# Attention scores from rounded parts: three one-pass products in place of one fp32 product, in a two-block transformer kernel on one Trainium2 core

## The chip, the core and the metric

The kernel runs on one core of one Trainium2 chip. The metric is the device time of one execution in microseconds (us), lower is better. Engines are called as in the profile: PE is the matrix engine (TensorE), PEld its weight loads, DVE the vector engine, ACT the scalar engine, POOL the GpSimd engine, SP the engine whose queue issues most of the DMAs.

## What is computed

The reference is a chain of two transformer blocks on a sequence of 512 tokens with 1024 channels, all in fp32: an attention layer with forget gates and 16 heads of 64 (the "first attention"), an attention layer with a sliding window, then a second block with three mixers and an MLP. The change touches one product of the first attention, the logits:

```python
u = rmsnorm(h, norm_a_g[i])
proj = u @ w_in_a[i]
q, k, v, f_logit, gate = jnp.split(proj, ...)
q = rmsnorm(q.reshape(b, s, N_HEADS_A, HEAD_DIM), qnorm_a_g[i])
k = rmsnorm(k.reshape(b, s, N_HEADS_A, HEAD_DIM), knorm_a_g[i])
...
logits = jnp.einsum('bqhd,bkhd->bhqk', qi, k) * scale
logits = logits + ci[..., :, None] - c_k[..., None, :]
logits = jnp.where(causal, logits, -jnp.inf)
p = jax.nn.softmax(logits, axis=-1)
return jnp.einsum('bhqk,bkhd->bqhd', p.astype(v.dtype), v)
```

## The kernel before

Everything is kept transposed in SBUF: channels on the 128 partitions, the 512 tokens along the free dimension. The kernel is written by hand, one instruction stream for each engine, with semaphores between them; so the order of the work on an engine is the order in which its function calls the helpers.

A projection is done in units. A unit is 128 output channels: 8 contraction tiles of 128, and for each three products, because both operands are split into a rounded part (type fp32r, which PE multiplies in one pass) and a rest (the value less its rounded part, also fp32r): high by high, high by low, low by high (`gemm`, L868 to L870). The weights of a unit are loaded by SP, rounded by ACT (`split_hi`, L1953) and their rest is formed by DVE (`split_lo`, L2456) or POOL (L498).

The first attention works on pairs of heads, n = 0 to 7; head 0 of a pair lies on partitions 0 to 63, head 1 on 64 to 127. For each pair m four units are projected: queries, keys, values, gate. DVE scales them out of PSUM (`scale_a`, L1203); ACT squares the queries and keys (L1993), PE sums the squares within a head, ACT and DVE form the inverse root (`root_scalar`, L576 to L579; `rsqrt_vector`, L584 and L586), and DVE multiplies by it (`normed_a`, L926), into `qn` and `kn`, the two halves of tile `qkv`. The semaphore `a_qk` counts these. Then come the scores, in three rounds (`scores_a`, L995 and L998): round 0 is query block 3 against 512 keys, round 1 query block 2 against 384 keys, round 2 query block 1 against 256 keys and query block 0 against 128. Each round writes one PSUM bank for each head, `S[0]` and `S[1]`:

```python
A_ROUND = [[(3, 0, 4 * P)], [(2, 0, 3 * P)], [(1, 0, 2 * P), (0, 2 * P, P)]]
mm(S[h][:, at:at + w], qn[lo:hi, q * P:(q + 1) * P], kn[lo:hi, 0:w], start=(i == 0), stop=False)
```

The operands of this product are fp32 with 64 contraction rows. A bf16 product adds the causal mask (L998). DVE adds the forget gate's terms and takes the lowest value of each row (`logits_a`, L1010), ACT takes the exponentials (`exps_a`, L1023), PE transposes them (`turn_a`, L1035), ACT copies the transposes out of PSUM (`take_turned_a`, L1046), and PE multiplies them by the values (`mix_a`, L1056).

While PE works on the scores of pair n it also projects pair n + 1: between two steps of the attention always stands half a unit (4 contraction tiles, 12 products) or two halves. The order on PE for a pair is: half a unit; scores round 0; two halves; scores round 1; transposes of round 0; half a unit; mixing of round 0; half a unit; scores round 2; transposes of round 1; half a unit; mixing; half a unit; transposes of round 2; half a unit; mixing; spreading of the softmax's sums (`spread_a`, L1078); transposing the values (`turn_v`, L1436). In the last pair, n = 7, there is no next pair to project; only the gate's unit and the first units of the output projection (`output_a`) stand between the steps.

On ACT the end of a pair is: `root_scalar` for the keys of pair n + 1, `take_turned_a(n, 2)`, `split_hi` of a unit, and the DMA of the forget gate's terms for a later pair (`load_c`). On DVE it is: `normed_a` for the queries of pair n + 1 behind `logits_a(n, 2)`, `scale_a` for the values, a `split_lo`, `normed_a` for the keys, another `split_lo`, and a piece of other work: in pairs 0 to 3 a part of the rotary angles, in pairs 4 to 7 a block of the second block's modulation (`ada_block`, L985). The next pair on DVE begins with `scale_a` of the gate's unit, the copy of the transposed values (L2535), a `split_lo`, and `logits_a` of round 0. Pair 0 has a preamble of its own, in which the same steps stand without a previous pair.

`normed_a` writes `qn` and `kn` in place, one buffer each. So it waits until the scores of the previous pair are done (`a_scores` at 6 m).

## Time and profile before

| | |
|---|---|
| runs | 1260.44 us median of 3 (1259.88 to 1260.48) |
| profiled execution | span 1259.4 us; 1.0 us below the median of the runs, which also holds what lies around the span |
| PE | busy 1244.9 us, 99% of the span |
| DVE, ACT, POOL | busy 56%, 53%, 29% |
| first attention's pairs | scores of pair 0 begin at 39.3 us, those of pair 7 at 269.1 us; 33.2 us for a pair |

How to read it: PE is called busy from the first to the last of its matmuls' records, and a matmul's record is longer than its share of the engine, since matmuls are pipelined. So the time that a matmul costs is read from the distance between the starts of two that follow each other, not from its duration. DVE and ACT records also overlap a little with the next one. Every time below is counted from the span's start.

### The profile page before, as it was taken

To read this page: it belongs to the slowest core of one execution; us is meant where nothing else is said; L and a number is where in the kernel's file an instruction comes from. 1 tells how busy PE (TensorE), PEld (TensorE's weight loads), DVE (VectorE), ACT (ScalarE), POOL (GpSimd) and SP (SyncE) were. 2 spreads that over 40 slices of the span, in tenths; PEclk is the share of its full clock that TensorE was granted. 3 is DMA by queue.
4 is the path that set the end of the run, shared out by engine and by line. 5 is a ranking of instruction groups with operands and counts; after the bars stand their busy time and mean duration, and the time that the engine had idled before them with its cause. 6 is when DMAs were issued, how large, how long until landed. Compare 5 with 4: busy or idle time off the path is not lost.

```text
span 1259.4 us, 19239 instructions
## 1 busy us (share of the span) xinstructions
PE 1244.9 (99%) x7192; PEld 1003.7 (80%) x7192; DVE 702.1 (56%) x1486; ACT 672.4 (53%) x1278; POOL 370.2 (29%) x191
## 2 busy tenths in 40 slices
PE   9999999999999999999999999999999999999998
PEld 8777777778877777689676888888988888888887
DVE  6766667775575766565798546684662121221223
ACT  6766666675437676635567886753542242331331
POOL 0000000004310000054487774123255344353450
PEclk9999999999999999999999999999999999999999
DMA  5322243343332322253222022331363233232232
GB/s 204 107 67 85 84 158 126 119 134 117 100 90 97 101 84 85 83 184 92 68 84 84 18 68 69 117 135 50 102 217 116 71 115 101 84 109 92 84 100 68
DMA packets 38411, 128.11 MB, mean 102 GB/s; under 512 B 4640, under 2 KB 7584, under 8 KB 38320
## 3 DMA queue, kind: packets, MB, share of 16 engines
q1 hardware_dynamic: 35792, 121.91, 30.3%
q10 hardware_dynamic: 2528, 4.98, 1.1%
q8 instruction: 58, 0.95, 0.3%
q14 instruction: 33, 0.27, 0.1%
HBM read 123.43 MB, written 2.13 MB: 100 GB/s over the span
## 4 chain that ended last, share of the span: by engine, by line
PE 80%; ACT 6%; issue 6%; DVE 5%; DMA 1%; POOL 1%; ACTq 0%; DVEq 0%; SPq 0%; POOLq 0%
PE G L868 19%; PE G L870 19%; PE G L869 19%; ACT scr L1249 2%; PE S L1708 2%; PE S L995 2%; PE O L1056 2%; DVE wL L2456 1%; PE T L1035 1%; ACT wH L1953 1%; DMA w<-weights_dram 1%; PE S L1726 1%; PE N L1078 1%; PE G L840 1%; PE G L841 1%
## 5 line engine op out<-in xcount | busy, mean ns | idle before, releaser
L498 POOL TENSOR_TENSOR wL<-w,wH 128x1024 fp32r<-128x1024 f32 x119 | 290.2, 2443 | 831.1 <-ACT wH L1953 831.0
L868 PE MATMUL G<-hi,wH 128*128 128x512 f32 x1208 | 487.1, 403 | 0.5 <-DVE xT L963 0.4
L870 PE MATMUL G<-hi,wL 128*128 128x512 f32 x1208 | 472.5, 391 | 0.0
L869 PE MATMUL G<-lo,wH 128*128 128x512 f32 x1208 | 472.1, 391 | 0.0
L868 PEld LDWEIGHTS G<-hi,wH 128*128 128x128 f32 x1208 | 227.6, 188 | 56.6 <-issue 9.7
L1953 ACT ACTIVATE wH<-w 128x1024 fp32r<-128x1024 f32 x170 | 179.2, 1055 | 170.6 <-PE G L870 111.3
L870 PEld LDWEIGHTS G<-hi,wL 128*128 128x128 f32 x1208 | 227.3, 188 | 49.9
L869 PEld LDWEIGHTS G<-lo,wH 128*128 128x128 f32 x1208 | 228.0, 189 | 44.8 <-issue 1.2
L965 DVE SCALAR_TENSOR_TENSOR xT<-G,modT,xT 128x512 f32<-128x512 f32 x34 | 25.5, 751 | 124.9 <-PE G L870 124.9
L2456 DVE TENSOR_TENSOR wL<-w,wH 128x1024 fp32r<-128x1024 f32 x51 | 62.3, 1222 | 42.3 <-ACT wH L1953 41.5
L2428 ACT ACTIVATE tmp<-G 128x512 f32<-128x512 f32 x31 | 18.6, 600 | 119.7 <-PE G L870 116.1
L2981 DVE TENSOR_TENSOR T<-tmp,G 128x512 f32<-128x512 f32 x31 | 21.6, 696 | 94.5 <-ACT tmp L2428 94.5
L985 DVE CUSTOM_DVE_ANT_0 adaw<-adaw,scr 128x1024 f32<-128x1024 f32 x31 | 51.1, 1649 | 1.9 <-issue 1.7
L1023 ACT ACTIVATE scr<-scr,sa 128x256 f32<-128x256 f32 (+2 forms) x64 | 35.2, 558 | 26.9 <-DVE sa L1010 26.9
L1249 ACT ACTIVATE scr<-S,bs,bq 128x128 f32<-128x128 f32 (+1 forms) x64 | 33.6, 534 | 21.5 <-DVE bs L1239 21.5
L2985 DVE TENSOR_TENSOR lo<-T,hi 128x512 fp32r<-128x512 f32 x32 | 22.1, 692 | 26.5 <-ACT hi L2435 26.5
L2809 DVE TENSOR_TENSOR kd<-S,qkv 128x512 f32<-128x512 f32 x24 | 16.5, 689 | 31.1 <-ACT S L2256 27.1
L1010 DVE CUSTOM_DVE_ANT_0 scr<-S,kd 128x256 f32<-128x256 f32 (+2 forms) x64 | 28.6, 487 | 0.0
L1046 ACT ACTIVATE scr<-T 128x384 f32<-128x384 f32 (+1 forms) x48 | 22.7, 526 | 10.4 <-PE T L1035 9.9
L533 POOL TENSOR_TENSOR tmp<-tmp,rms 128x482 f32<-128x482 f32 (+19 forms) x20 | 24.4, 1222 | 11.2 <-ACT rms L2173 11.2
L2774 DVE MAX8 best<-adaw 128x8 f32<-128x256 f32 (+2 forms) x48 | 26.7, 557 | 0.8
L533 POOL TENSOR_TENSOR tmp<-tmp,rinv 128x482 f32<-128x482 f32 (+19 forms) x20 | 23.8, 1190 | 7.8 <-ACT rinv L2173 7.8
(461 smaller groups left out, 1923.9 us busy)
## 6 DMA issues: line engine op xcount, KB each, us to landing
w<-weights_dram SPq DMA_DIRECT2D x170, 512.0 KB, 3.6
adaw<-ada_dram SPq DMA_DIRECT2D x43, 512.0 KB, 4.3
kd<-c_dram ACTq DMA_DIRECT2D x8, 512.0 KB, 3.7
cbias<-ada_dram SPq DMA_DIRECT2D x5, 512.0 KB, 4.3
xT<-x_dram SPq DMA_DIRECT2D x4, 512.0 KB, 8.0
out_dram<-xT SPq DMA_DIRECT2D x8, 256.0 KB, 2.6
scr<-ca_dram SPq DMA_DIRECT2D x2, 512.0 KB, 4.9
kd<-cbias SPq DMA_DIRECT2D x8, 128.0 KB, 3.2
```

The source lines that it names most:

```text
L498: g.tensor_tensor(wL[:, u.slot], w32[:, u.slot % 2], wH[:, u.slot].bitcast(f32), ALU.subtract).then_inc(w_lo, 1)
L533: g.tensor_tensor(cacc[:, n % 2, back:SEQ], cacc[:, n % 2, back:SEQ], term[n % 3][:, 0:SEQ - back], ALU.add).then_inc(sem("conv_added"), 1)
L868: mm(home[:, :], whi, H[:, k, :], start=(k == first), stop=False)
L869: mm(home[:, :], whi, L[:, k, :], start=False, stop=False)
L870: last = mm(home[:, :], wlo, H[:, k, :], start=False, stop=(k == final))
L985: v.tensor_tensor_reduce(out=home, in0=home, in1=copy, scale=1.0, scalar=0.0, op0=ALU.mult, op1=ALU.add, accum_out=modsum[:, b.n:b.n + 1]) ...
L1010: v.tensor_tensor_reduce(out=slot[:, h * 512 + at:h * 512 + at + w], in0=S[h][:, at:at + w], in1=kd[:, n % 2 * 2 + h, 0:w], scale=-1.0, sc ...
L1023: s.activation(part, part, ACT.Exp, bias=sa[:, n % 2, LOW, h, q:q + 1], scale=-1.0, accum_out=sa[:, n % 2, ASUM, h, q:q + 1]).then_inc(sem ...
L1249: s.activation(pb[:, h * 512 + at:h * 512 + at + w], S[h][:, at:at + w], ACT.Exp, bias=st[:, NEGM, h, q:q + 1], scale=bq[:, n % 2, ROOT, h ...
L1953: s.activation(wH[:, u.slot], w32[:, u.slot % 2], ACT.Copy).then_inc(w_hi, 1)
L2456: v.tensor_tensor(wL[:, u.slot], w32[:, u.slot % 2], wH[:, u.slot].bitcast(f32), ALU.subtract).then_inc(w_lo, 1)
L2774: link(v.max(best[:, n % 2, :], part))
```

## The change

Each fp32 product of the scores becomes three products of fp32r operands, added up in the same PSUM bank: rounded queries by rounded keys, rests of the queries by rounded keys, rounded queries by rests of the keys. The product of the two rests is left out.

The rounded parts and the rests are made in two new tiles, `qk_hi` and `qk_lo` (128 x 2 x 512 each; index 0 the queries, 1 the keys). ACT rounds (`qk_high`), DVE subtracts (`qk_low`). `normed_a` no longer waits for the scores of the previous pair but for the rounding of it (`a_qk_hi`); the rounding waits for the scores (`a_scores`). PE waits for the last rest (`a_qk_lo`) in place of `a_qk`. The room for the two tiles comes from the area that is reserved for the descriptors of software-made DMAs, which is set to 1024.

```diff
+        qk_hi, qk_lo = sb("qk_hi", [P, 2, SEQ], f32r), sb("qk_lo", [P, 2, SEQ], f32r)
...
         def scores_a(pe, n, r):
-            pe.wait_ge(sem("a_qk"), 2 * n + 2)
+            pe.wait_ge(sem("a_qk_lo"), 2 * n + 2)
             wait(pe, sem("a_logits"), 8 * n + 2 * r)
             for i, (q, at, w) in enumerate(A_ROUND[r]):
-                for h in range(2):
-                    lo, hi = h * DH, (h + 1) * DH
-                    mm(S[h][:, at:at + w], qn[lo:hi, q * P:(q + 1) * P], kn[lo:hi, 0:w], start=(i == 0), stop=False)
+                for part, (a_q, a_k) in enumerate(((qk_hi, qk_hi), (qk_lo, qk_hi), (qk_hi, qk_lo))):
+                    for h in range(2):
+                        lo, hi = h * DH, (h + 1) * DH
+                        mm(S[h][:, at:at + w], a_q[lo:hi, 0, q * P:(q + 1) * P], a_k[lo:hi, 1, 0:w], start=(i == 0 and part == 0),
+                           stop=False)
...
+        def qk_high(act, m, which):
+            act.wait_ge(sem("a_qk"), 2 * m + which + 1)
+            wait(act, sem("a_scores"), 6 * m)
+            s.activation(qk_hi[:, which, :], [qn, kn][which], ACT.Copy).then_inc(sem("a_qk_hi"), 1)
+
+        def qk_low(dve, m, which):
+            dve.wait_ge(sem("a_qk_hi"), 2 * m + which + 1)
+            v.tensor_tensor(qk_lo[:, which, :], [qn, kn][which], qk_hi[:, which, :].bitcast(f32), ALU.subtract
+                            ).then_inc(sem("a_qk_lo"), 1)
...
             root_scalar(act, link, "a", 0, 1)
+            qk_high(act, 0, 0)
...
             load_c(0)
             split_a(2)
+            qk_high(act, 0, 1)
             load_c(1)
...
                     root_scalar(act, link, "a", n + 1, 1)
+                    qk_high(act, n + 1, 0)
                 take_turned_a(act, n, 2)
                 if more:
                     split_a(6 + 4 * n)
+                    qk_high(act, n + 1, 1)
...
             def normed_a(m, which, src, dst):
-                normed_vector(dve, link, "a", m, which, src, dst, which, mark("a_scores", 6 * m), sem("a_qk"))
+                normed_vector(dve, link, "a", m, which, src, dst, which, mark("a_qk_hi", 2 * m - 1 + which), sem("a_qk"))
...
             split_a(2)
+            qk_low(dve, 0, 0)
+            qk_low(dve, 0, 1)
...
                     normed_a(n + 1, 1, kraw, kn[:, :])
+                    qk_low(dve, n + 1, 0)
                     split_a(6 + 4 * n)
+                    qk_low(dve, n + 1, 1)
...
-    nc = bacc.Bacc("TRN2", target_bir_lowering=False, num_devices=1)
+    nc = bacc.Bacc("TRN2", target_bir_lowering=False, num_devices=1, dynamic_dma_scratch_size=1024)
```

The order on DVE ahead of the first scores, before (`normed_a` of the keys of pair 0 is the row with `kraw`; wL is the weights' rest, `cact` a small vector; line numbers of the profile):

```order
L926 SCALAR_TENSOR_TENSOR qkv<-kraw,vecT,rinv 128x512 [waits dve_link]
L2526 TENSOR_TENSOR cact<-vecT,cth 128x8 [waits c_sigmoid]
L2456 TENSOR_TENSOR wL<-w,wH 128x1024 [waits gemm_done,w_hi]
L2529 CAST pair_r<-pair 128x128 [waits const_here]
L2535 COPY qkv<-T 128x512 [waits a_vturn,dve_link]
```

And now:

```order
L927 SCALAR_TENSOR_TENSOR qkv<-kraw,vecT,rinv 128x512 [waits dve_link]
L2543 TENSOR_TENSOR cact<-vecT,cth 128x8 [waits c_sigmoid]
L2473 TENSOR_TENSOR wL<-w,wH 128x1024 [waits gemm_done,w_hi]
L1011 TENSOR_TENSOR qk_lo<-qkv,qk_hi 128x512 [waits a_qk_hi] x2
L2548 CAST pair_r<-pair 128x128 [waits const_here]
L2554 COPY qkv<-T 128x512 [waits a_vturn,dve_link]
```

The first scores used to be free once the first of these rows was done; now they are free behind both rests, which stand after a split of weights.

The order on DVE at the end of pair 6, from the keys of pair 7 on, before:

```order
L926 SCALAR_TENSOR_TENSOR qkv<-kraw,vecT,rinv 128x512 [waits a_scores,dve_link]
L2456 TENSOR_TENSOR wL<-w,wH 128x1024 [waits gemm_done,w_hi]
L984 MEMSET stat 128x1 [waits ada_here0,cactb_here]
L985 ISA adaw,modsum<-adaw,cbias 128x1024
L985 ISA modsum 128x1
L1203 TENSOR_TENSOR zraw<-G,tmp 128x512 [waits a_silu,gemm_done]
L2535 COPY qkv<-T 128x512 [waits a_vturn]
L2456 TENSOR_TENSOR wL<-w,wH 128x1024 [waits gemm_done,w_hi]
L882 SCALAR_TENSOR_TENSOR th<-zraw,th 128x512 [waits a_softplus]
```

And now (behind the last row `logits_a(7, 0)` follows in both):

```order
L927 SCALAR_TENSOR_TENSOR qkv<-kraw,vecT,rinv 128x512 [waits a_qk_hi,dve_link]
L1011 TENSOR_TENSOR qk_lo<-qkv,qk_hi 128x512 [waits a_qk_hi]
L2473 TENSOR_TENSOR wL<-w,wH 128x1024 [waits gemm_done,w_hi]
L1011 TENSOR_TENSOR qk_lo<-qkv,qk_hi 128x512 [waits a_qk_hi]
L985 MEMSET stat 128x1 [waits ada_here0,cactb_here]
L986 ISA adaw,modsum<-adaw,cbias 128x1024
L986 ISA modsum 128x1
L1216 TENSOR_TENSOR zraw<-G,tmp 128x512 [waits a_silu,gemm_done]
L2554 COPY qkv<-T 128x512 [waits a_vturn]
L2473 TENSOR_TENSOR wL<-w,wH 128x1024 [waits gemm_done,w_hi]
L883 SCALAR_TENSOR_TENSOR th<-zraw,th 128x512 [waits a_softplus]
```

Two instructions of 512 columns have come in ahead of everything that DVE does for pair 7, one of them behind a wait for ACT.

The first scores on PE, before:

```order
L995 MATMUL S<-qkv 128x512 [waits a_qk]
L995 MATMUL S<-qkv 128x512
L998 MATMUL S<-band,identb 128x128 x2
```

And now:

```order
L997 MATMUL S<-qk_hi 128x512 [waits a_qk_lo]
L997 MATMUL S<-qk_hi 128x512
L997 MATMUL S<-qk_hi,qk_lo 128x512 x2
L997 MATMUL S<-qk_lo,qk_hi 128x512 x2
L1001 MATMUL S<-band,identb 128x128 x2
```

One product of each head has become three, and the two heads alternate within each.

## Rows read from the trace of the kernel before

**Rows 1.** The page: busy time of the engines, and PE's granted clock in 40 slices.

```profile
PE 1244.9 (99%) x7192; PEld 1003.7 (80%) x7192; DVE 702.1 (56%) x1486; ACT 672.4 (53%) x1278; POOL 370.2 (29%) x191
PEclk9999999999999999999999999999999999999999
```

**Rows 2.** Busy time by stretch: us, PE, PEld, DVE, ACT, POOL, clock, DMA; one pair.

```profile
72.00:105.00 33.00, 33.00 (x197) 25.25 (x195) 22.26 (x52) 22.13 (x44) 0.00 (x0) 1.00 0.25 81
```

**Rows 3.** Timeline of PE in pair 1: start us, busy us, engine, line; three rounds of scores.

```profile
72.54 0.30 PEld L995 LDWEIGHTS S<-qkv 64*128 64x128 f32 x4 [0.35 <-issue]
72.54 1.13 PE L995 MATMUL S<-qkv 64*128 64x512 f32 x4
73.60 0.28 PE L998 MATMUL S<-band,identb 128*128 128x128 bf16 x2
...
74.02 0.39 PE L869 MATMUL G<-lo,wH 128*128 128x512 f32 x1
74.25 0.39 PE L870 MATMUL G<-hi,wL 128*128 128x512 f32 x1
...
79.35 0.92 PE L995 MATMUL S<-qkv 64*128 64x384 f32 x4
80.20 0.29 PE L998 MATMUL S<-band,identb 128*128 128x128 bf16 x2
...
88.47 0.92 PE L995 MATMUL S<-qkv 64*128 64x256 f32 x8
89.33 0.40 PE L998 MATMUL S<-band,identb 128*128 128x128 bf16 x4
```

**Rows 4.** Timeline of PE elsewhere: fp32r products of 256 columns, transposes of 128.

```profile
80.32 1.04 PE L1035 MATMUL T<-ident,scr 128*128 128x128 f32 x8
...
570.97 0.28 PE L840 MATMUL G<-hi,wH 128*128 128x256 f32 x1
571.09 0.28 PE L841 MATMUL G<-hi,wL 128*128 128x256 f32 x1
```

**Rows 5.** Timeline ahead of the first scores: ACT, DVE and PE.

```profile
36.50 1.06 ACT L1953 ACTIVATE wH<-w 128x1024 fp32r<-128x1024 f32 x1 [0.16 <-issue]
...
38.27 0.75 DVE L926 SCALAR_TENSOR_TENSOR qkv<-kraw,vecT,rinv 128x512 f32<-128x512 f32 x1
...
39.02 1.22 DVE L2456 TENSOR_TENSOR wL<-w,wH 128x1024 fp32r<-128x1024 f32 x1
...
39.30 1.13 PE L995 MATMUL S<-qkv 64*128 64x512 f32 x4
40.15 0.22 DVE L2529 CAST pair_r<-pair 128x128 fp32r<-128x128 f32 x1
```

**Rows 6.** Groups by line and shape: the same rounding and subtraction elsewhere; busy, mean ns.

```profile
L943 ACT ACTIVATE hi<-og 128x512 fp32r<-128x512 f32 x16 | 10.1, 633 | 22.8 <-DVE og L1401 20.0 <-DVE og L1087 2.8
L947 DVE TENSOR_TENSOR lo<-og,hi 128x512 fp32r<-128x512 f32 x16 | 11.0, 686 | 1.4 <-ACT hi L943 1.4
```

**Rows 7.** Timeline at the end of pair 2: keys of pair 3, and its scores.

```profile
98.72 0.75 DVE L926 SCALAR_TENSOR_TENSOR qkv<-kraw,vecT,rinv 128x512 f32<-128x512 f32 x1
...
105.77 1.13 PE L995 MATMUL S<-qkv 64*128 64x512 f32 x4
```

**Rows 8.** Timeline from the keys of pair 7 to its last scores: DVE, ACT, PE.

```profile
264.85 0.75 DVE L926 SCALAR_TENSOR_TENSOR qkv<-kraw,vecT,rinv 128x512 f32<-128x512 f32 x1
...
269.25 0.69 DVE L2535 COPY qkv<-T 128x512 f32<-128x512 f32 x1 [0.55 <-PE T L1436]
...
273.06 0.71 ACT L1023 ACTIVATE scr<-scr,sa 128x512 f32<-128x512 f32 x1
...
274.22 1.04 PE L1035 MATMUL T<-ident,scr 128*128 128x128 f32 x8
...
278.11 0.55 DVE L1010 CUSTOM_DVE_ANT_0 scr<-S,kd 128x384 f32<-128x384 f32 x1
...
278.98 0.92 PE L995 MATMUL S<-qkv 64*128 64x256 f32 x8
```

## The prediction

> **What bounds the kernel now.** I read the page first. PE is busy for 99% of the span and its granted clock is full, 2.4 GHz, in all 40 slices [rows 1]; no other engine passes 56%. Then the stretch of one pair of heads: PE is busy for all of its 33 us, DVE for 22.3, ACT for 22.1 [rows 2]. So in the first attention every us that PE's work loses is a us of the kernel, and every us that PE is made to wait is one too; work on DVE and ACT costs nothing as long as nobody on PE waits for it. The rest is therefore three questions: what the scores cost on PE, at which of the eight pairs PE would wait for the new steps, and what lies hidden.
>
> **The products on PE.** The two heads of a pair lie on different halves of the rows, and their products run side by side: four records, each longer than half a us, fit into 1.13 us [rows 3]. What counts is the distance from the first score to the mask's product behind it: 1.06 us in round 0 (73.60 less 72.54), 0.85 in round 1 (80.20 less 79.35), 0.86 in round 2 (89.33 less 88.47) [rows 3]. Rounds 0 and 1 differ by 128 columns and 0.21 us, 1.64 ns a column, which is four columns' time at 2.4 GHz (0.417 ns): an fp32 product streams its columns four times. What is left, 1.06 less 512 x 1.64 ns, is 0.2 us a round that doesn't depend on the columns: 0.1 ahead of it, 0.1 behind.
>
> The new product is three one-pass products. Their price is bounded from two sides. At best each costs one pass, 0.417 ns a column, so each round saves one pass of its columns: 0.21 us, 0.16 us, and in round 2 (384 columns) 0.16. At worst each costs what an fp32r product with all 128 rows costs now from start to start: 0.23 us for 512 columns [rows 3], 0.12 for 256 [rows 4], so about 0.175 for 384, and for 128 columns 0.11, the step of the transposes of 128 columns ((1.04 less 0.27, the length of one) / 7) [rows 4]. With 0.2 us around them that makes 0.89, 0.73 and 0.89 us: savings of 0.17, 0.12 and -0.03. So a pair saves between 0.26 and 0.53 us. I take 0.20, 0.15 and 0.02, **0.37 us a pair**: the small parts of round 2 are nearest to the rows with 0.12 and 0.11, the wide ones lie between, since the first gap and the last hold one pass each and not a whole step.
>
> The transposes' step shows that 128 columns cost 0.11 us, twice their columns' time. The Trainium skill has another number: on its page "TensorE: Matmul & The Clock Gate", section "Back-to-back issue gap", the gap of a single warm matmul is its columns at 2.4 GHz and 2.5 ns, which gives 56 ns at 128 columns. By that round 2 would save 0.16 us more a pair and the sum below would be lower by about 1.1 us; the rows decide here.
>
> **The new steps on ACT and DVE.** Sixteen roundings of 0.63 us on ACT and sixteen subtractions of 0.69 us on DVE [rows 6], 1.3 and 1.4 us for a pair of 33.2 in which each has some 11 us free [rows 2]. In the middle pairs they are hidden: the keys of pair 3 are ready at 99.47 and its scores begin at 105.77 [rows 7], 6.3 us later. Behind the keys now come a rest (0.7), a split of weights that already stood there (1.2) and a second rest (0.7), and ACT rounds the keys (0.6) while DVE splits; ready some 2.5 us after the keys, 3.8 us ahead of need. Pairs 1 to 6 cost PE nothing, I say. ACT's transposes' copy behind the rounding of the queries moves by 0.1 us at most, since ACT waited half a us for PE there.
>
> **Pair 0** has no such slack. The keys are ready at 39.02 and PE starts the scores at 39.30, as soon as its previous product lets it [rows 5]. Now DVE first splits weights from 39.02 on, as before; the instruction behind the split starts at 40.15 [rows 5], and that is now the first rest; the second follows after 0.61 to 0.69 us and takes 0.69. So the last rest is there at 41.45 to 41.55. ACT is no later: it splits at 36.5 for 1.06 us [rows 5], 0.6 later than that now, is free by 38.2, and rounds the keys from 39.06 to 39.7. PE starts at about 41.5 in place of 39.30: **2.2 us lost** (2.1 to 2.5), nothing is behind it that PE could take up meanwhile, because its stream is in order. DVE's copy of the values and ACT's later work are not late by that: they are ahead of a PE that is itself 2.2 us later.
>
> **Pair 7** is the other tight place, since PE has little to do between its steps. The two rests push DVE by 1.2 us from 265.6 on. DVE had some waits there, 0.55 us for PE's transposes [rows 8] among them, but the gate's chain over ACT (from `zraw`) runs beside that wait and isn't absorbed as far; I reckon that `logits_a(7, 0)` comes 0.8 us later. Before, the exponentials ended at 273.8 (with the read of their sum 273.9) and the transposes began at 274.22, right behind PE's own work [rows 8]: slack 0.35. PE now arrives 0.35 us sooner (its savings in rounds 0 and 1), so it waits 0.8 us: those savings are gone and 0.45 us more. Next, the logits of round 1 ended at 278.7 and the scores of round 2 began at 278.98 [rows 8]; DVE is 0.8 later and PE 0.45, another 0.1. Behind that DVE waits for PE again. **Pair 7 loses 0.5 us** against before (0.1 to 0.9), and gains only the 0.02 of round 2.
>
> **Edits at nothing.** The smaller area for DMA descriptors: POOL has no DMA of its own in this program, so no queue changes. The wait of `normed_a` for the roundings of the previous pair in place of its scores: both are over long before. SP's and POOL's streams are untouched; the DMAs that ACT issues (`load_c`) stand behind the rounding of the keys and move by about 1.5 us, with a whole pair in which to land. If the cover in pairs 1 to 6 were gone, each would cost what it is late by.
>
> **The sum.** Seven pairs save 0.37 us, 2.6 in all; pair 0 gives back 2.2, pair 7 0.5. Against the profiled execution: 1259.4 - 2.6 + 2.2 + 0.5 = 1259.5 us span, and the median of the runs lies 1.0 above the span: **1260.5 us, no change**. The bounds: 7 x 0.53 saved against 2.1 and 0.1 lost gives -1.5; 7 x 0.26 against 2.5 and 0.9 gives +1.6. So 1258.9 to 1262.1.
>
> **The rivals.**
>
> *The halves don't run side by side in this type.* No row has fp32r products with 64 rows. If the two heads' products came one after another, each round would hold six in place of three: 6 x 0.23 and 0.2 is 1.58 against 1.06, 6 x 0.175 and 0.2 is 1.25 against 0.85, 6 x 0.12 + 6 x 0.11 and 0.2 is 1.58 against 0.86: 1.64 us more a pair. Times eight, and 2.2 for pair 0 (pair 7's waits vanish in it): +15.3, **1275.7 us, slower**. It decides as soon as the two heads' starts lie a step apart. Against it speaks that fp32, and the same kernel's other products on part of the rows, do run side by side. Chance 0.08.
>
> *Weight loads that can't run ahead.* An fp32 product is two loads and two matmuls. All four loads of round 0 take 0.30 us in all, while its matmuls run for 1.06 [rows 3]: the second loads are done before the second matmuls start. If fp32r's loads had to wait for the matmul on the same rows, two loads in round 0, two in round 1 and five in round 2 would stand bare, at about 0.1 us each (half of the 0.2 us around a round): 0.9 us a pair, +7.2 on the sum less the 0.5 that pair 7 then hides: **1267.2 us, slower**. The Trainium skill has this rule, same page, section "The mechanism": weight loads overlap running matmuls only on other row groups. The trace of the fp32 scores disagrees with it, by the 0.30 us. Chance 0.07.
>
> *Narrow fp32r products cost more than one pass.* Nothing in the trace is fp32r and narrower than 256 columns. If the 128 columns of round 2 cost four passes each as fp32 does, 0.21 in place of 0.11, a pair costs 0.3 us more: +2.4, **1262.9 us**, on the border of slower. Chance 0.06.
>
> *The wait at pair 0 is shorter.* If ACT and DVE overlap better than the starts say, and every product costs one pass, the saving may come through: 8 x 0.53 less 1.5 is -2.7, **1257.7 us, faster**. The split at 39.02 would have to be quicker than in each of its other records. Chance 0.05.
>
> *The clock falls.* The granted clock is full throughout [rows 1], and PE never pauses for 2 us once it has begun; the pause at pair 0 is new. Products at 1.2 GHz take twice as long; a few us of them would cost 2 to 3 us: **1263 us**. Chance 0.04.
>
> **How the numbers follow.** The forecast has 0.70. A measurement of this kernel can tell about 0.2% from no change, 2.5 us, so 1257.9 to 1263.0 is "the same". Within it lie the forecast's bounds, and about half of the third and the last rival. Faster: 0.05 and a little for errors in my waits, 0.06. Slower: 0.08 + 0.07 + half of 0.10, and the same for errors, 0.21. Same: 0.73. The range takes in the forecast and its bounds, the narrow products and the clock: 1258.2 to 1263.4, some 0.8 of the chance; only the two large slower cases and the ends lie outside.
>
> **What would show it.** Right: the distance from the first score to the mask's product falls to about 0.86, 0.70 and 0.84 us, with six records side by side; a wait of about 2.2 us of PE for `qk_lo` ahead of the first scores and for no other pair; about 32.9 us for a pair; a wait of 0.8 us of PE for ACT at 7's first transposes. Wrong: a round 0 of more than 1.06 us; starts of the two heads more than 0.1 us apart; a PE wait for `qk_lo` in pairs 1 to 7; a clock slice below full.

## The result, and the profile after

The changed kernel takes 1263.32 us (median of 18 runs, 1259.52 to 1267.46); the kernel before took 1260.47 us beside it (18 runs, 1258.47 to 1262.62). The ratio is 1.0025, 95% interval 1.0015 to 1.0034: **slower by 0.25%**, 3.2 us. Three more measurements of the unedited change (below) gave 1.0007, 1.0010 and 1.0011, so its mean over four is 1.0013, 1.7 us; the first was the highest of them. The profiled execution has a span of 1262.0 us at a mean granted clock of 0.996. Two executions of later experiments fell into a slow state (1903 and 1544 us, at clocks of 0.60 and 0.75) and are in no ratio or mean below.

The page of the changed kernel, answering to [rows 1]:

```profile
PE 1243.2 (99%) x7256; PEld 1008.3 (80%) x7256; DVE 711.8 (56%) x1502; ACT 680.3 (54%) x1294; POOL 370.0 (29%) x191
PEclk9999999999999999999999999999999999999999
```

PE is busy 1.7 us less than before in a span that is 2.6 us longer. The products are cheaper, then, and PE stands idle more.

**The products.** Timeline of PE and PEld in the changed kernel, pair 1 (columns as in [rows 3]); L997 are the scores, L1001 the mask:

```profile
74.47 0.50 PE L997 MATMUL S<-qk_hi 64*128 64x512 f32 x2
74.57 0.19 PEld L997 LDWEIGHTS S<-qk_hi,qk_lo 64*128 64x128 f32 x2
74.80 0.39 PE L997 MATMUL S<-qk_hi,qk_lo 64*128 64x512 f32 x2
75.03 0.39 PE L997 MATMUL S<-qk_lo,qk_hi 64*128 64x512 f32 x2
75.36 0.29 PE L1001 MATMUL S<-band,identb 128*128 128x128 bf16 x2
...
81.08 0.45 PE L997 MATMUL S<-qk_hi 64*128 64x384 f32 x2
...
81.81 0.28 PE L1001 MATMUL S<-band,identb 128*128 128x128 bf16 x2
...
90.07 0.39 PE L997 MATMUL S<-qk_hi 64*128 64x256 f32 x2
90.30 0.28 PE L997 MATMUL S<-qk_hi,qk_lo 64*128 64x256 f32 x2
90.41 0.27 PE L997 MATMUL S<-qk_lo,qk_hi 64*128 64x256 f32 x2
90.53 0.22 PE L997 MATMUL S<-qk_hi 64*128 64x128 f32 x2
90.58 0.27 PE L997 MATMUL S<-qk_hi,qk_lo 64*128 64x128 f32 x2
90.69 0.28 PE L997 MATMUL S<-qk_lo,qk_hi 64*128 64x128 f32 x2
90.90 0.40 PE L1001 MATMUL S<-band,identb 128*128 128x128 bf16 x4
```

From the first score to the mask: 0.89 us in round 0, 0.73 in round 1, 0.83 in round 2, where [rows 3] had 1.06, 0.85 and 0.86. Each "x2" is the two heads in one row, side by side. The first scores of pairs 1, 2 and 6 start at 74.47, 107.34 and 238.87: a pair takes 32.88 us ((238.87 less 74.47) / 5), where it took 33.23 (105.77 less 72.54, [rows 3, 7]; 105.77 is where pair 2 begins, not pair 3). That is 0.35 us saved a pair.

**The waits.** The same kernel's waits of PE from the start to 290 us (total, times, longest), and the timeline around them:

```profile
PE S L997 <- DVE qk_lo L1011: 2.1, 1, 2.1
PE N L1421 <- DVE epsc L2477: 1.1, 1, 1.1
PE S L997 <- DVE sa L1023: 0.7, 1, 0.7
```

```profile
39.05 1.22 DVE L2473 TENSOR_TENSOR wL<-w,wH 128x1024 fp32r<-128x1024 f32 x1
39.09 0.63 ACT L1007 ACTIVATE qk_hi<-qkv 128x512 fp32r<-128x512 f32 x1 [1.26 <-DVE qkv L927]
...
40.19 1.29 DVE L1011 TENSOR_TENSOR qk_lo<-qkv,qk_hi 128x512 fp32r<-128x512 f32 x2
...
41.53 0.50 PE L997 MATMUL S<-qk_hi 64*128 64x512 f32 x2 [2.13 <-DVE qk_lo L1011]
...
273.42 0.08 DVE L1023 DVE_READ_ACCUMULATOR2_ANT sa<- 128x1 f32 x1
...
273.65 0.44 PE L997 MATMUL S<-qk_hi 64*128 64x384 f32 x2 [0.66 <-DVE sa L1023]
...
274.49 1.04 PE L1048 MATMUL T<-ident,scr 128*128 128x128 f32 x8
...
279.40 0.39 PE L997 MATMUL S<-qk_hi 64*128 64x256 f32 x2
```

Pair 0's scores begin at 41.53 in place of 39.30 [rows 5], 2.23 us late, and `qk_lo` is waited for once in the whole kernel. (The 1.1 us at L1421 is in the kernel before too, under L1408.) In pair 7 PE waits 0.66 us for the logits of round 0 ahead of the scores of round 1. The scores of pair 7's round 2, the last that the change touches, begin at 279.40, where they began at 278.98 [rows 8]: **0.4 us late. The rest of the 2.6 us in this trace arises behind the first attention**, in work that the change doesn't touch.

Most of it arises at PE's sums of squares behind the output of the second attention. The waits of PE between 560 and 570 us, of the kernel before and of the changed one:

```profile
PE N L680 <- DVE rms L663: 0.2, 1, 0.2
```

```profile
PE N L681 <- DVE rms L664: 1.7, 1, 1.7
```

And the timeline of POOL, DVE and ACT ahead of them, again before and then changed:

```profile
559.17 2.74 POOL L498 TENSOR_TENSOR wL<-w,wH 128x1024 fp32r<-128x1024 f32 x1 [1.26 <-ACT wH L1953]
...
560.35 2.65 DVE L985 CUSTOM_DVE_ANT_0 adaw<-adaw,scr 128x1024 f32<-128x1024 f32 x1 [0.69 <-issue]
```

```profile
558.78 1.22 DVE L986 CUSTOM_DVE_ANT_0 adaw<-adaw,scr 128x1024 f32<-128x1024 f32 x1
...
560.15 1.06 ACT L1966 ACTIVATE wH<-w 128x1024 fp32r<-128x1024 f32 x1 [4.09 <-DMA w<-weights_dram]
...
561.29 2.41 POOL L499 TENSOR_TENSOR wL<-w,wH 128x1024 fp32r<-128x1024 f32 x1 [3.24 <-ACT wH L1966]
561.42 3.36 DVE L986 CUSTOM_DVE_ANT_0 adaw<-adaw,scr 128x1024 f32<-128x1024 f32 x1 [1.41 <-issue]
```

ACT waits 4.09 us for weights there. DVE's sum over a block of the modulation vector begins 1.1 us later, and beside POOL's subtraction it takes 3.36 us; the same instruction took 1.22 at 558.78. PE waits 1.7 us for what stands behind it, 1.5 more than before. Three more traces of the change (experiments 2, 11 and 14) have 3.4 us for this sum as well. In the first two of them it begins at 559.88 and 560.11, and PE waits 0.5 us. What is special to the trace here is the late start, behind the weights that ACT waited for.

With 0.4 and 1.5 us, 0.7 of the 2.6 are left. By the starts of the same products, the changed kernel is 2.1 us late at 815 us and 2.9 at 868; between the two PE's clock fell to 1.2 GHz at 860 us here, and at 823 in the trace of before. The second trace of the kernel before (experiment 1) has its fall at 857 too: against the first it is 0.4 us early at 815 and 0.4 late at 868, the same 0.8. So these 0.8 us are the place of a fall, which moves without the change as well.

### The profile page after: what moved, and what is told of

The parts are those of the page before. It is cut to its first block, busy times and chain, and to the rows that moved or that the text cites. A ratio compares the mean times of both kernels' runs of the same rounds, so it can differ in the third digit from the quotient of the medians.

```text
span 1262.0 us, 19413 instructions
## 1 busy us (share of the span) xinstructions
PE 1243.2 (99%) x7256; PEld 1008.3 (80%) x7256; DVE 711.8 (56%) x1502; ACT 680.3 (54%) x1294; POOL 370.0 (29%) x191
## 4 chain that ended last, share of the span: by engine, by line
PE 79%; ACT 7%; DVE 7%; issue 5%; POOL 1%; DMA 1%; ACTq 0%; DVEq 0%; POOLq 0%
PE G L869 19%; PE G L871 18%; PE G L870 18%; ACT scr L1262 2%; PE O L1069 2%; PE S L997 1%; PE S L1721 1%; PE T L1048 1%; DVE wL L2473 1%; ACT wH L1966 1%; PE S L1739 1%; PE N L1421 1%; POOL tmp L534 1%; PE G L841 1%; PE G L842 1%
## 5 line engine op out<-in xcount | busy, mean ns | idle before, releaser
L2796 DVE MATCH_REPLACE8 adaw<-best,adaw 128x256 f32<-128x256 f32 (+2 forms) x48 | 26.0, 543 | 0.0
```

## The experiments

All ratios are to the kernel before on the same chip, with their 95% intervals; us are the ratio times 1260.5.

**1 and 2: both kernels again, unedited.**

> The kernel before, once more, to have the granted clock of each of its executions. In the two traces the first attention differs by only 0.4 us, yet the medians differ by 2.9, and the executions of the changed kernel have clocks from 0.998 down to 0.994, the lower the longer. Theory 1 (the pause): the wait of 2.2 us at pair 0 lets the clock fall in part of the executions; then the kernel before has no execution below about 0.996, and its times lie within 1258.5 to 1262.6. Theory 2 (chance elsewhere: the clock falls later, near 730 to 860 us, whatever the first attention does): the kernel before shows 0.994 as often as the changed one, in about a third of its executions.

> The changed kernel once more. Ratio 1.0025 +- 0.001, clocks again between 0.998 and 0.994, with about 2 us for each 0.002. Theory 1: an execution of 0.994 has a stretch at half clock within some 10 us of the pause at 39 to 41.5 us, beside two later ones. Theory 2: none there. The wait of 1.7 us for DVE at 564 us (rms, L664) that the profile of the changed kernel shows and that of the kernel before doesn't: if it comes from where a load happens to land, it is there in one of two executions of either kernel; if it comes from the change, it is there again.

The kernel before: 0.9998 (0.9989 to 1.0007). Theory 1 wanted no execution of it below a clock of about 0.996, theory 2 wanted a third of them there. Of these 11 two are, of all 124 executions of the kernel before beside the experiments 14, of the change's 53 also 14: neither theory holds as it was put. The change: 1.0007 (0.9996 to 1.0017), its trace again with 2.1 us for `qk_lo` and 0.7 for `sa`; the wait at 565 us was 0.5 us in it, not 1.7. So that wait differs between executions of one kernel.

**3: the pause alone.** Pair 0's roundings, rests and PE's wait for them, put into the kernel before; all products stay fp32.

```diff
+            if n == 0:
+                pe.wait_ge(sem("a_qk_lo"), 2)
...
+            qk_low(dve, 0, 0)
+            qk_low(dve, 0, 1)
```

> The kernel before with the two new tiles, the smaller descriptor area and, for pair 0 alone, the two roundings and the two rests; PE waits for the last rest ahead of pair 0's first scores. All products stay fp32. Theory 1: span + 2.2 us for the pause and clocks down to 0.994 as in the changed kernel, some 2 us more in the middle: ratio about 1.0035. Theory 2: + 2.2 us alone and clocks as before: 1.0018.

Ratio 1.0025 (1.0014 to 1.0035), 3.2 us for a wait of 2.2 us in the trace: one us more than the trace puts at the pause, and between the two forecasts.

**4: the pause filled with products that nobody reads.** 9 fp32 products of 128 columns ahead of pair 0's first scores.

```diff
+                if n == 0:
+                    for _ in range(9):
+                        mm(T[1][:, 0:P], ones[:, :], ones[:, :], start=True, stop=True)
                 scores_a(pe, n, 0)
```

> The changed kernel with nine more products of ones (128 columns, fp32, into a bank that nobody reads then) on PE ahead of pair 0's scores, about 2.0 us of work in the place of the pause; they add no result. Theory 1: the pause is gone for the clock though not for the time: the first attention costs the same, and the executions at 0.994 vanish: ratio about 1.0003. Theory 2: the same 1.0025 as the changed kernel.

Ratio 0.9997 (0.9988 to 1.0006), though the scores begin at 41.53 as in the change.

**5: the tiles alone**, with nothing written to them, and the smaller descriptor area, in the kernel before.

> The kernel before with nothing but the two new tiles (unused) and the smaller area for DMA descriptors: memory layout alone. So far, executions of equal granted clock are some 1.3 us longer in the changed kernel, of which the trace puts 0.4 us into the first attention; the rest could be the wait of PE at 564 us (0.7 to 2.0 us in four traces with the new layout, 0.44 in two without). Theory 1 (the layout makes loads land later or DVE and POOL slower at 540 to 564 us): ratio 1.0007, and that wait is above 0.6 us. Theory 2 (chance of when loads land): ratio 1.0000 within 0.0008, wait 0.44.

Ratio 0.9999 (0.9990 to 1.0009), wait at 565 us 0.2 us as before: the layout costs nothing.

**6: the pause filled with useful work.** The second half of pair 1's query unit is moved ahead of pair 0's first scores.

```diff
-                    gemm_a(n + 1, 0, FIRST if n else range(2, 4))
+                    gemm_a(n + 1, 0, FIRST if n else range(2, KT))
...
-                    gemm_a(n + 1, 0, SECOND)
+                    if n:
+                        gemm_a(n + 1, 0, SECOND)
                     gemm_a(n + 1, 1, FIRST)
```

> The changed kernel with the second half of the queries' unit of pair 1 moved on PE from behind to ahead of pair 0's first scores: 12 products of 0.23 us, 2.7 us of real work in the 2.2 us pause. If the sum of the terms is right, the pause is gone and with it 2.2 us: first attention 0.4 - 2.2 = 1.8 us shorter than before, ratio 0.9986. If the changed kernel's loss lies elsewhere, it keeps +0.9 and the ratio is 0.9993. If the pause only moves (the scores' consumers are late instead), PE waits ahead of round 1.

Ratio 1.0004 (0.9995 to 1.0012). The trace does what was expected: no wait of PE for `qk_lo`, and round 2 of pair 7 at 277.20, 1.8 us ahead of before. The times don't show it. In its trace 0.6 us go again between 565 and 596 us, and PE runs at 1.2 GHz for longer around 735 us (granted clock of 730 to 745 us: 0.77, before 0.89). Over its 12 executions the mean granted clock is 0.9958, where the kernel before beside it has 0.9971: an estimate from this, 0.0013 of 1259 us, is 1.6 us lost to more stretches at 1.2 GHz, out of the 2.3 us that are missing. Both forecasts of the time missed. Why the clock falls more often here, where PE has no pause ahead of the scores, is **not explained**.

**7: pair 0 stays fp32**, without its roundings and rests.

```diff
+            if n == 0:
+                pe.wait_ge(sem("a_qk"), 2)
+            else:
+                pe.wait_ge(sem("a_qk_lo"), 2 * n)
```

> The changed kernel with pair 0's scores as fp32 products again, without roundings and rests for pair 0. The pause of 2.2 us goes, pair 0's saving of 0.35 goes too: first attention 0.4 - 2.2 + 0.35 = 1.45 us shorter than before, ratio 0.9988 (0.9995 if something outside keeps 0.9).

Ratio 0.9987 (0.9978 to 0.9996), 1.6 us faster than before; round 2 of pair 7 begins at 277.46, 1.5 us ahead.

**8: work in the pause as in 6, and pair 7 in fp32**, without its roundings and rests.

> fill_gemm with pair 7's scores as fp32 products, and no roundings and rests for pair 7. Seven pairs save 0.35 us each and nothing is given back: 2.4 us shorter than before, ratio 0.9981. If pair 7's waits are not from the two rests on DVE, it is like fill_gemm less the saving: 0.9989.

Ratio 0.9988 (0.9980 to 0.9997). Its trace has no wait of PE for `sa`, and round 2 of pair 7 at 276.42, 2.6 us ahead of before: the wait in pair 7 comes from that pair's roundings and rests, and goes with them. The times again keep less, 1.5 us: they fit the forecast for the case that the wait has another cause (0.9989), and the trace speaks against that case. Here the mean clock, 0.9969 against 0.9971, doesn't explain the difference.

**9 and 10: the modulation blocks spread evenly**, in the change and in the kernel before.

```diff
-ADA_PER = {"b": (ADA_OB, (0, 1, 1, 1, 1, 2))}
+ADA_PER = {"b": (ADA_OB, (1, 1, 1, 1, 1, 1))}
```

> The change, with one edit far behind it: the six blocks of the modulation vector that VectorE sums beside the output of the second attention are spread evenly (one per output tile, where the last tile had two and the first none), so that at 558 to 565 us one block instead of two stands ahead of the add that TensorE's sums wait for. In the traces taken so far that wait is 0.2 us in kernels that save time ahead of it or change nothing, 1.7, 0.5, 1.2 and 0.4 us in those with the change's pause. Theory A (the rest of the loss lies in this wait, which the first attention's 0.4 us only sets off): the wait reads about 0.2 us, the ratio to the kernel before is 1.0003, and the trace is less than 1 us behind that of before at 600 us. Theory B (the loss has another home, stretches at 1.2 GHz that come more often): the wait is gone as well, but the ratio stays at 1.001 to 1.0025. Theory C (nothing systematic lies behind the first attention): ratio 1.0003 here and for the change run again.

> The kernel before with the same edit of the blocks alone. It has 0.2 us of that wait to lose, so all theories expect no difference that can be measured: ratio 0.9995 to 1.0003. A slower time would say that the even spread costs something of its own (a load of a block waited for, earlier in the output), which would then have to be taken off the result of the run above.

The change so edited: 1.0013 (1.0002 to 1.0024); the kernel before so edited: 1.0002 (0.9992 to 1.0011). The wait at the sums is gone in both, but an earlier block now holds up a sum that PE needs; the waits of PE between 530 and 570 us have this row in the changed kernel and its like in the other:

```profile
PE G L869 <- DVE xT L964: 1.3, 1, 1.3
```

So one wait took the place of another, and theory A, by which the rest of the loss is that wait at 565 us, isn't supported. It isn't refuted either, since a wait of the same size was left; in the kernel before, 1.3 us of it cost 0.3 us by the ratio, which is within the noise. What this trace shows beside it is new. Its timeline of PE has the first scores at 41.5 us as before, but these stretches (columns as in [rows 2], the clock third from the end):

```profile
40.00:42.00 2.00, 0.51 (x4) 0.46 (x6) 1.97 (x5) 0.94 (x1) 0.00 (x0) 1.00 0.91 276
42.00:43.00 1.00, 1.00 (x7) 0.37 (x6) 1.00 (x2) 0.12 (x1) 0.00 (x0) 0.51 0.55 153
43.00:44.00 1.00, 1.00 (x4) 0.81 (x4) 1.00 (x5) 0.00 (x0) 0.00 (x0) 0.50 0.84 344
44.00:45.00 1.00, 1.00 (x4) 0.81 (x3) 0.67 (x5) 0.91 (x3) 0.00 (x0) 0.50 0.74 115
```

**Right behind the pause PE ran at 1.2 GHz.** Round 2 of pair 7 began at 280.86 here, 1.5 us later than in the change's first trace.

**11: the change a third time.**

> The change itself once more, unedited. Two measurements gave ratios of 1.0025 and 1.0007. Theory A and theory B of the run above: about 1.0015. Theory C: 1.0003, which the interval should then hold. The trace should again show +2.2 us at the first scores, about 33.2 minus 0.35 per pair after it, +0.4 at 560 us, and a wait of 0.4 to 1.7 us at the half sums of the second attention's output.

Ratio 1.0010 (0.9997 to 1.0022); full clock behind the pause, wait of 0.5 us at 565.

**12: the change for pairs 1 to 6 alone**; pairs 0 and 7 keep fp32 scores.

```diff
-            pe.wait_ge(sem("a_qk_lo"), 2 * n + 2)
+            if n in (0, 7):
+                pe.wait_ge(sem("a_qk"), 2 * n + 2)
+            else:
+                pe.wait_ge(sem("a_qk_lo"), 2 * n)
```

> The change for pairs 1 to 6 alone: pairs 0 and 7 keep their fp32 scores, and their roundings and rests are left out. All theories: no wait at 40 us, none of 0.56 us ahead of round 1 of pair 7, six pairs at 0.35 us: the trace is 2.1 us ahead of before at 290 us and at 560 us, ratio 0.9983 (1258.4 us). Against pair 0 alone in fp32 (1258.6 us, 1.7 ahead at 290 us) it should be 0.4 us better, which the trace can show and the times hardly.

Ratio **0.9983 (0.9975 to 0.9992)**, 2.1 us faster than before, as forecast; its median, 1259.44 us, is 1.4 us below that of the kernel before beside it. Round 2 of pair 7 begins at 277.05, 1.9 us ahead. It has the lowest ratio of the study, but its interval overlaps with that of experiment 7 (0.9978 to 0.9996), so the times don't show which of the two is faster; in both, time and lead at pair 7 agree.

**13: a longer pause.** Four discarded operations of the size of a rest between the two rests of pair 0.

```diff
+            dve.wait_ge(sem("a_qk_hi"), 2)
+            for _ in range(4):
+                link(v.tensor_tensor(qk_lo[:, 1, :], kn, qk_hi[:, 1, :].bitcast(f32), ALU.subtract))
             qk_low(dve, 0, 1)
```

> The change with four more operations of the size of a rest (0.6 us each) on VectorE between the two rests of pair 0, whose results are thrown away, so that TensorE pauses about 2.4 us longer ahead of the first scores. Theory A (a pause costs its length and nothing else): the time is that of the change plus 2.4 us, ratio 1.0033 (between 1.0013 and 1.0044 plus what the interval leaves open), and the granted clock reads 1.00 from 42 to 48 us. Theory B (the clock can fall to 1.2 GHz behind the pause, as it did in the trace with the even blocks, at 42.0 to 45.4 us with a granted clock of 0.50, where it cost 1.1 us more): a longer pause makes it likelier, so the trace shows 0.5 behind the pause, the mean clock is lower than in the change's own executions (0.9961 to 0.9967), and the ratio is 1.0040 or more.

Ratio 1.0042 (1.0029 to 1.0055), 5.3 us, mean granted clock of the executions 0.9948. Two theories stand against each other from here on: by A a pause costs its length and nothing else, by B the clock can fall behind it. The added operations wait for each other, and the first scores began at 44.37, 2.8 us later than in the change. The products behind them ran at 1.2 GHz from the first one on; busy time and clock by stretch, where the change's first trace has a clock of 1.00 in all three:

```profile
34.00:42.00 8.00, 5.34 (x26) 4.08 (x24) 7.82 (x12) 5.07 (x8) 0.00 (x0) 1.00 0.65 193
42.00:46.00 4.00, 1.63 (x7) 0.89 (x8) 3.86 (x7) 0.33 (x1) 0.00 (x0) 0.64 0.45 148
46.00:50.00 4.00, 4.00 (x13) 3.23 (x12) 1.68 (x7) 1.52 (x4) 0.00 (x0) 0.50 0.43 131
```

Round 1 of pair 7 begins at 279.01, 5.4 us later than in the change's first trace: 2.8 of pause, 2.5 of products at 1.2 GHz. With the change's 0.4 that is 5.8 us in this trace, 5.3 in the times. Theory A with the pause as it really was, 2.8 us more than in the change, on the change's mean of 1.7, would give 4.5, and the interval (3.7 to 6.9) holds that too. So the time alone doesn't tell the theories apart; the clock rows do, for B.

**14: the change a fourth time.**

> The change itself, unedited, beside the kernels of this call. Theory A: ratio 1.0003 to 1.0010. Theory B: about 1.0013, the mean of the ratios so far (1.0025, 1.0007, 1.0010), with a mean granted clock below that of before (0.9969).

Ratio 1.0011 (1.0001 to 1.0022); the profiled execution was the longest of the 12, 1265.63 us at a mean granted clock of 0.994. Its timeline behind the pause:

```profile
41.47 0.50 PE L997 MATMUL S<-qk_hi 64*128 64x512 f32 x2 [2.12 <-DVE qk_lo L1011]
...
42.47 0.64 PE L869 MATMUL G<-hi,wH 128*128 128x512 f32 x1
42.91 0.63 PE L870 MATMUL G<-lo,wH 128*128 128x512 f32 x1
43.34 0.63 PE L871 MATMUL G<-hi,wL 128*128 128x512 f32 x1
...
46.19 0.39 PE L869 MATMUL G<-hi,wH 128*128 128x512 f32 x1
46.42 0.39 PE L870 MATMUL G<-lo,wH 128*128 128x512 f32 x1
```

The same products take 0.43 us from start to start until 46 us and 0.23 behind it. Round 2 of pair 7 began at 280.90, 1.5 us later than in the first trace. The clock fell three times more, the first of these behind the wait at the sums (0.78 us here), not counting the last few us of the kernel, in which it falls in every trace; stretches by window:

```profile
568.30:571.60 3.30, 3.30 (x17) 3.30 (x17) 0.74 (x5) 0.47 (x2) 0.00 (x0) 0.50 0.00 0
738.90:742.30 3.40, 3.40 (x10) 2.66 (x9) 2.92 (x5) 2.99 (x5) 2.27 (x2) 0.51 0.03 7
861.80:865.20 3.40, 3.40 (x8) 1.97 (x7) 0.00 (x0) 1.20 (x3) 0.00 (x0) 0.50 0.00 0
```

**15 and 16: the filled pause and the bare pause once more.**

> The nine dummy products in the pause once more. They leave the pause's length (2.1 us at the first scores) as it is and keep TensorE busy in it. Theory A: the same as the change of this call. Theory B: better than the change of this call by the extra stretches at 1.2 GHz that are spared, ratio 0.9997 to 1.0005, mean granted clock 0.9970 or more.

> The kernel before with the roundings and rests of pair 0 and the wait for them, all products fp32, once more. The trace put 2.1 us at the pause and nothing else, the time 3.1 us. Theory A: ratio 1.0017 (2.1 us). Theory B: 1.0020 to 1.0025, mean granted clock below that of before.

Filled: 1.0003 (0.9994 to 1.0012). Its executions have a mean granted clock of 0.9965, below the 0.9970 that B had forecast (the kernel before beside it: 0.9970). The pause alone: 1.0030 (1.0019 to 1.0041), 3.8 us, above both forecasts, at a mean clock of 0.9959. The stretch from 42 to 46 us in the two, filled first:

```profile
42.00:46.00 4.00, 4.00 (x22) 3.10 (x19) 3.15 (x9) 1.58 (x5) 0.00 (x0) 1.00 0.70 243
```

```profile
42.00:46.00 4.00, 4.00 (x13) 2.92 (x12) 2.47 (x7) 1.54 (x5) 0.00 (x0) 0.61 0.69 238
```

All traces side by side. "Round 2" is the start of pair 7's round 2 less 278.98; "clock" the granted clock from 38 to 46 us; "wait" PE's at the sums near 565 us.

| kernel | round 2, us | clock | wait, us | ratio, in us |
|---|---|---|---|---|
| change, traces 1 to 3 | +0.4, +0.2, +0.25 | 1.00, 1.00, 1.00 | 1.7, 0.5, 0.5 | 3.2, 0.9, 1.3 |
| change, trace 4 | +1.9 | 0.79 | 0.8 | 1.4 |
| change, blocks even | +1.9 | 0.79 | 1.3, elsewhere | 1.6 |
| pause alone, twice | +2.1, +3.6 | 1.00, 0.81 | 0.4, 0.2 | 3.2, 3.8 |
| longer pause | +5.8 | 0.82 | 0.2 | 5.3 |
| filled pause, twice | +0.4, +0.2 | 1.00, 1.00 | 1.2, 0.5 | -0.4, +0.4 |
| pair 0 in fp32 | -1.5 | 1.00 | 0.2 | -1.6 |
| pairs 0 and 7 in fp32 | -1.9 | 1.00 | 0.2 | -2.1 |
| work in the pause | -1.8 | 1.00 | 0.3 | +0.5 |
| the same, pair 7 in fp32 | -2.6 | 1.00 | 0.2 | -1.5 |
| before, again | -0.1 | 1.00 | 0.2 | -0.3 |
| before, tiles alone | 0.0 | 1.00 | 0.2 | -0.1 |
| before, blocks even | +0.1 | 1.00 | 1.3, elsewhere | +0.3 |

The mean granted clock of all executions doesn't rest on single traces: 0.9969 for the kernel before (124 executions) and for the filled pause (22), 0.9964 for the change (53), 0.9960 for the pause alone (15), 0.9948 for the longer pause (5). That is the order of theory B, but 0.0005 is little, and experiment 6, at 0.9958 without a pause, shows that the clock depends on more than this pause.

## Why the prediction was wrong

It named the likeliest outcome as no change, at 1260.5 us. The change is slower by 0.25% in the first measurement and by 0.13% over four; both lie inside the range of 1258.2 to 1263.4, the first at its end.

**The sum for the first attention was right.** It said 0.37 us saved a pair; measured 0.35. By round: 0.20, 0.15, 0.02 forecast, 0.17, 0.12, 0.03 found, and a few hundredths at the changes between kinds of product. Pair 0: 2.2 forecast, 2.23 found, for the reason given (split of weights, then two rests). Pairs 1 to 6 don't wait. Together +0.1 forecast, +0.2 to +0.4 in three traces with the full clock. The small difference is the size of the saving.

**Pair 7 was right in size and wrong in place.** The forecast had 0.5 us lost, at the first transposes, for ACT. The trace has 0.6 (0.16 us ahead at its first scores, 0.42 behind at round 2). PE in fact waits ahead of round 1's scores for the logits of round 0, 0.66 us (no row of [rows 8] shows that instruction); I had put DVE's delay there at 0.8 us (measured 0.6) and not asked who waits for it first. Experiments 8 and 12, where the wait is gone, show that the pair's two rests cause it.

**The step that failed is the clock: the sum charges the pause its length and nothing behind it.** The rival "the clock falls" got 0.04. It doesn't fall in every execution, but in 3 of the 7 traces with the bare pause, and in the one with the longer pause; in none of the 10 traces without a pause or with it filled (two of the kernel before, eight of experiments). Price: 1.5 us (280.90 and 280.86 against 279.40; 3.6 against 2.1 in the pause alone), not the 2 to 3 that I gave it. That is some 0.65 us in the mean (3/7 x 1.5), an estimate from 7 traces. The filled pause is the test of it: the scores begin just as late, PE is busy, the clock stays at 2.4 GHz in both traces (too few to tell from 3 in 7), and over two measurements the ratio is 1.0000 against 1.0013 for the change. Where both ran side by side (experiments 2 and 4, 14 and 15) the change has 1.0007 and 1.0011, and its executions are 1.3 us longer in the mean both times (for the two together 0.4 to 2.1, an estimate from their scatter).

The times also say, without any theory of the clock, that the pause costs more than its length. The pause alone costs 3.2 and 3.8 us for 2.2 us of wait. Pair 0 put back in fp32 turns +1.7 into -1.6, 3.3 us, where the pause less the pair's saving is 1.9. That is 1.3 or 1.4 us beside the length both times, of which the fall of the clock behind the pause explains about half.

I had argued from the page that "the granted clock is full in all 40 slices". It isn't. The page shows tenths of a slice of 32 us, and a short fall doesn't lower the digit below 9. By stretches the kernel before has

```profile
734.40:737.70 3.30, 3.30 (x9) 2.57 (x9) 3.17 (x5) 3.30 (x6) 2.18 (x2) 0.50 0.00 0
823.20:826.50 3.30, 3.30 (x9) 2.54 (x8) 3.30 (x8) 1.29 (x3) 0.00 (x0) 0.50 0.23 45
```

and falls like these come in every kernel here, one to four in an execution, at places that change (569, 735, 780, 825 and 860 us). That the clock falls in this kernel without any such pause was there to be read, and would have made the rival worth far more than 0.04.

**What lies behind the first attention was taken as fixed.** PE's wait at the second attention's sums read 0.2 us before, and 0.2 or 0.3 again in the versions that lead by 1.5 us or more; in the change it was 1.7, 0.5, 0.5 and 0.8, in versions that are later still 0.4 (+2.1), 0.2 (+3.6) and 0.2 (+5.8). In one execution of the change the clock fell behind it as well (0.50 at 568 us, above). So part of the loss may be in how work for PE, DVE and POOL falls together after a small shift. Its mean size I can't give: 0.7 us more wait over four traces (3.5 / 4 less 0.2), but spreading the blocks only moved the wait.

The parts come to 1.65 us against a measured mean of 1.7: 0.3 in the first attention, 0.65 for the clock behind the pause, 0.7 at the sums. That they meet so closely is partly luck. The same sum gives the filled pause 0.3 and, from its waits of 1.2 and 0.5, 0.65, so about 1 us, where 0.0 was measured, within 0.8. The first part is read in traces and the fall of the clock is seen in them; its share and the third part aren't shown in size. The first measurement's 3.2 us stays partly open: 6 of its 18 executions had a mean granted clock of 0.994, as had trace 4 with its four falls and 1265.6 us. That theirs fell at the same places wasn't seen. Also open is why experiment 6 has more stretches at 1.2 GHz, and why experiment 8 kept 1.1 us less than its trace leads.

**The other rivals fell by their first row.** The heads run side by side (each row "x2", one start). Weight loads run ahead: the loads of the second product start at 74.57, 0.1 us behind the start of the first product and 0.23 ahead of their own, and the whole of round 2, with twelve loads, takes 0.83 us. The Trainium skill's rule ("TensorE: Matmul & The Clock Gate", "The mechanism"), that loads overlap matmuls only on other row groups, is contradicted by that again, since each head's next weights go to the same rows as its running product; by the prediction's estimate for this rival the kernel would have lost another 7 us. Narrow products aren't four passes: 128 columns step by 0.05 and 0.11 us (90.53, 90.58, 90.69). On the same page of the Trainium skill, "Back-to-back issue gap" gives 56 ns for 128 columns when alone, and 81 ns in a stream of loads and products, which the prediction left out; here the first step agrees with the 56 and the next is twice that, their mean is 0.08 us. So neither the 56 ns nor my 0.11 held for all of them.

"Within 0.2% is the same" was also too wide for what followed: with 18 runs on each side the interval was 0.1% on either side, and 0.25% could be told from nothing.

## What to carry to other kernels

A change that makes one product cheaper on an engine that is 99% busy is worth its saving only where its new preparation is hidden; here six of eight pairs gave 0.35 us each and the two ends gave back more than all of them. Leaving the ends as they were made 1.0013 into 0.9983. A pause of 2 us on PE can cost more than its length, 3.2 and 3.8 us for one of 2.2 here: look at the granted clock in stretches of a few us behind it and in several executions, and if the pause can't go, put products into it.

## What the runs showed that was not expected

- The clock falls behind a pause of only 2.1 to 2.2 us of a PE that was busy until then, in 3 traced executions of 7; behind one of 5.0 us in the one trace taken. A fall costs 1.5 to 1.6 us where 512-column products follow (0.43 us for each instead of 0.23).
- Nine products of constants that nobody reads make the kernel faster: 1.0000 in place of 1.0013, the means of two and four measurements, or 1.0009, the mean of the two that ran beside them.
- One and the same instruction of DVE (128x1024, multiply and sum) takes 1.22 us alone. Where it starts while a subtraction of POOL's runs, its record grows by about the time that is left of that: 3.36 us with 2.28 beside POOL, 1.35 with 0.26.
- At equal work the executions of one kernel differ by up to 8 us (1259.5 to 1267.5 for the change), and the mean granted clock goes with it: in the first measurement of the change, executions at 0.998 took 1261.2 us in the mean and those at 0.994 took 1266.3.
